# Output's first tile and first weight block prepared during attention's last steps, and one meeting of engines per stage change

## The reference, cut to what matters

```
h = concat(meta, x)                                  # 2064 x 1024
u = rms_norm(h) * norm_w
q, k, v, sb_gate, z, xbc, dt = split(u @ w_in)
o_sb  = stick_breaking_attention(q, k, v) * silu(sb_gate)
o_ssd = ssd_chunked(silu(conv(xbc)), dt, ...) * silu(z)
y = concat(rms_norm(o_sb) * sb_w, rms_norm(o_ssd) * ssd_w)   # 2048 wide
h = h + y @ w_out
out = rms_norm(h) * final_w                          # without the meta rows
```

## Time and profile before

| | us |
|---|---|
| median of 3 runs (2681.78 to 2683.33) | 2683.29 |
| the profiled execution, its own time | 2685.85 |
| its span, first to last instruction | 2683.9 |
| mean granted TensorE clock | 0.974 of full |
| PE busy | 2548.6 (95%) |
| DVE, ACT, POOL busy | 1688.8, 1347.1, 1552.1 |

### The profile page before, as it was taken

One profiled execution on the slowest core, in us unless ns is written; L12 is line 12 of the kernel. 1 busy time (PEld: TensorE's weight loads), 2 busy tenths in 40 slices (PEclk: granted clock), 3 DMA queues, 4 the chain that ended last, 5 costly groups with the idle time before them and its releaser, 6 DMA issues. The chain is left out here.

```text
span 2683.9 us, 41154 instructions
## 1 busy us (share of the span) xinstructions
PE 2548.6 (95%) x14100; PEld 1797.4 (67%) x14100; DVE 1688.8 (63%) x2064; ACT 1347.1 (50%) x2096; POOL 1552.1 (58%) x1253
## 2 busy tenths in 40 slices
PE   4999999998999999899899999999999999599998
PEld 3788777776888888766555555555555555488887
DVE  5522556635213455177688889888888987655554
ACT  4433333344333333344378778777877876322221
POOL 5876666688777777578666666565666655000000
PEclk7999999998999999999899999999999999799999
DMA  2443323333333333266712121212212111523230
GB/s 106 157 139 123 126 97 119 108 103 120 133 125 112 128 122 130 75 158 183 230 40 80 40 88 36 84 56 64 80 40 88 32 40 52 168 88 111 79 111 35
DMA packets 204101, 268.74 MB, mean 100 GB/s; under 512 B 13441, under 2 KB 137665, under 8 KB 197265
## 3 DMA queue, kind: packets, MB, share of 16 engines
q1 hardware_dynamic: 203920, 266.43, 31.0%
HBM read 169.36 MB, written 97.03 MB: 99 GB/s over the span
## 5 line engine op out<-in xcount | busy, mean ns | idle before, releaser
L2012 POOL TENSOR_TENSOR a_w<-a_beta,a_rest 128x1024 f32<-128x1024 f32 (+2 forms) x320 | 560.4, 1751 | 355.5 <-DVE a_rest L1969 209.3
L764 POOL TENSOR_TENSOR f_l_lo<-f_wst,f_l_hi 128x512 fp32r<-128x512 f32 x312 | 405.3, 1302 | 269.1 <-ACT f_l_hi L632 268.8
L1969 DVE TENSOR_TENSOR_SCAN a_rest<-a_keep,a_rest,a_ones 128x513 f32<-128x513 f32 x384 | 469.7, 1260 | 10.8 <-ACT a_keep L1939 10.8
L1889 PE MATMUL a_turn<-a_ident,a_w 128*128 128x128 f32 (+1 forms) x2432 | 343.6, 279 | 7.3 <-DVE a_wt L1923 6.1
L1904 PE MATMUL a_o<-a_wt,a_v 128*64 128x512 f32 (+3 forms) x1408 | 340.3, 562 | 8.9 <-DVE a_out L1979 8.9
L500 PE MATMUL f_xz<-f_t_hi,f_l_hi 128*128 128x512 f32 x832 | 330.2, 397 | 7.0 <-issue 4.4
L1923 ACT COPY a_wt<-a_turn 128x512 f32<-128x512 f32 (+3 forms) x440 | 225.1, 528 | 209.2 <-PE a_turn L1889 207.6
L500 PE MATMUL f_xz<-f_t_hi,f_l_lo 128*128 128x512 f32 x832 | 326.4, 392 | 0.0
L500 PE MATMUL f_xz<-f_t_lo,f_l_hi 128*128 128x512 f32 x832 | 326.0, 392 | 0.0
L1889 PEld LDWEIGHTS a_turn<-a_ident,a_w 128*128 128x128 f32 (+1 forms) x2432 | 257.6, 140 | 91.5 <-issue 65.4
L1939 ACT ACTIVATE a_keep<-a_z 128x1024 f32<-128x1024 f32 (+4 forms) x352 | 300.0, 852 | 4.5 <-PE a_z L1872 4.5
(11 more groups left out here) (256 smaller groups left out, 4272.5 us busy)
## 6 DMA issues: line engine op xcount, KB each, us to landing
f_wst<-in_w_pairs SPq DMA_DIRECT2D x52, 1024.0 KB, 5.8
scratch_gate<-f_out SPq DMA_DIRECT2D x64, 256.0 KB, 2.4
o_g<-scratch_mixed SPq DMA_DIRECT2D x32, 512.0 KB, 5.5
scratch_xbc<-f_out SPq DMA_DIRECT2D x36, 256.0 KB, 2.1
scratch_q_hi<-f_out SPq DMA_DIRECT2D x32, 256.0 KB, 3.3
scratch_q_lo<-f_out SPq DMA_DIRECT2D x32, 256.0 KB, 3.7
scratch_v<-f_out SPq DMA_DIRECT2D x32, 256.0 KB, 2.3
s_xc<-scratch_xbc SPq DMA_DIRECT2D x16, 512.0 KB, 5.8
```

Source lines behind the costliest of these rows:

```text
L764: return nc.gpsimd.tensor_tensor(out, a, b, op).then_inc(done, 1)
L1889: mm = nc.tensor.transpose(turn[h][0:rows, qi * P:(qi + 1) * P], tile[:, h, x:x + rows], ident[:, :])
L1969: mm = nc.vector.tensor_tensor_scan(rest[r % RS][:, h, tn - 1::-1], top, ones[:, 0:1].to_broadcast([P, tn]), start, ALU.mult, ALU.min)
L2012: nc.gpsimd.tensor_tensor(w[r % AS][:, :, 0:tn], beta[r % KEEPS][:, :, 0:tn], rest[r % RS][:, :, 1:tn + 1], ALU.mult).then_inc(w_ready, 1)
```

## The change

- **Meetings.** `start` no longer ends in a barrier: each engine raises its share and goes on; POOL then clears the semaphores that former stages left behind (`Memory.past`). At a stage's end they are only put on that list; the front stage alone (`at_once`) still clears and meets at its end. After output a clear and a meeting stand once.
- **Tile 0 of output in attention.** `OutputEarly` gets the tiles for it: high and low parts of g, a sum tile, the norm weights, high and low parts of one weight block. In the steps after the last score ACT squares the two halves (into the fourth staging tile) and takes a weight block's high part and both halves' high parts; DVE sums the two halves and takes the weight block's low part; POOL, after its last weights, multiplies both halves by the norm weights and takes their low parts. SP loads three weight blocks early instead of four, the norm weights with them, and two more blocks after the last chunk's store.
- **Order of weights.** Blocks come in the order 8 to 15, 0 to 7 (`place`), g's halves in the order 1, 0, and the first tile's products likewise. Block 8 is the one prepared early.
- **Output's opening.** Blocks 1 to 15 in that order; ACT squares tile 1 after the ninth, all else of tile 1's front comes after the last block, and its sums over blocks after `back(0, 0)`. Each half has its own `squares` tile.
- **Sums of squares** on PE stand between the first and second 48 matmuls of a tile, but for tile 0.

```
+    past = []
+
+    def __init__(self, nc, ctx, at_once=False):
+        self.nc, self.ctx, self.semaphores, self.at_once = nc, ctx, [], at_once
+        ctx.callback(self.leave)
 
     def start(self):
 
@@ -62,11 +64,21 @@
         engines = (nc.sync, nc.gpsimd, nc.scalar, nc.vector, nc.tensor)
         for n, sem in enumerate(self.semaphores):
             engines[n % len(engines)].sem_inc(sem, START)
-        nc.all_engine_barrier()
-
-    def clear(self):
-        self.nc.clear_and_free_semaphores(self.semaphores)
-        self.nc.all_engine_barrier()
+        Memory.clear(nc)
+
+    def leave(self):
+
+        Memory.past.extend(self.semaphores)
+        if self.at_once:
+            Memory.clear(self.nc)
+            self.nc.all_engine_barrier()
+
+    @staticmethod
+    def clear(nc):
+
+        if Memory.past:
+            nc.clear_and_free_semaphores(Memory.past)
+        Memory.past = []
...
-        m_ = Memory(nc, ctx)
+        m_ = Memory(nc, ctx, at_once=True)
...
                     late.load_first(sp)
+            sp.wait_ge(late.reduced[0][0], 1)
+            late.load_weight(sp, len(late.staging) - 1)
+            sp.wait_ge(late.w_high, 1)
+            sp.wait_ge(late.w_low, 1)
+            late.load_weight(sp, len(late.staging))
             for r in range(2):
                 sp.wait_ge(stored[r], START + 16 * CH // 2)
...
                 if n < N:
                     sigmoids(n)
+                if n == N:
+                    late.square(act, 1)
+                if n == N + 1:
+                    late.weight_high(act)
+                if n == N + 2:
+                    late.square(act, 0)
+                if n == N + 3:
+                    late.high(act, 1)
+                if n == N + 5:
+                    late.high(act, 0)
...
+                if n == N:
+                    late.reduce(dve, 1)
+                if n == N + 2:
+                    late.weight_low(dve)
+                if n == N + 3:
+                    late.reduce(dve, 0)
...
+            late.weigh(pool, 1)
+            late.weigh(pool, 0)
+            late.low(pool, 1)
+            late.low(pool, 0)
...
+        self.staging = self.h + self.y
+        self.squares = self.staging[-1]
         self.w_loaded = self.sems("o_w_loaded", len(self.staging))
...
+    def load_weight(self, sp, j):
+        r = j % len(self.staging)
+        sp.dma_start(self.staging[r][:, :], self.w_out[:, (j + KB) % MB, :]).then_inc(self.w_loaded[r], 16)
 
     def load_weights(self, sp):
-        for k in range(len(self.staging)):
-            self.load_weight(sp, k)
+        sp.dma_start(self.gw[:, :], self.group_w).then_inc(self.gw_loaded, 16)
+        for j in range(len(self.staging) - 1):
+            self.load_weight(sp, j)
 
     def load_g(self, sp, s, i):
-        for q in range(2):
+        for q in (1, 0):
...
+    def square(self, act, q):
+        act.wait_ge(self.g_loaded[0][q], 16)
+        if q == 0:
+            act.wait_ge(self.reduced[0][1], 1)
+        self.nc.scalar.activation(self.squares[:, :], self.half_of(self.g[0], q).rearrange("p b t -> p (b t)"), ACT.Square).then_inc(self.squared[0][q], 1)
+
+    def weight_high(self, act):
+        act.wait_ge(self.w_loaded[0], 16)
+        self.nc.scalar.activation(self.first_hi[:, :], self.staging[0][:, :], ACT.Copy).then_inc(self.w_high, 1)
+
+    def weight_low(self, dve):
+        dve.wait_ge(self.w_high, 1)
+        self.nc.vector.tensor_tensor(self.first_lo[:, :], self.staging[0][:, :], self.first_hi[:, :].bitcast(F32),
+                                     ALU.subtract).then_inc(self.w_low, 1)
+
+    def reduce(self, dve, q):
+        dve.wait_ge(self.squared[0][q], 1)
+        self.nc.vector.tensor_reduce(self.sq_sum[0][:, q, :],
+                                     self.squares[:, :].rearrange("p (b t) -> p t b", b=KB),
+                                     mybir.AxisListType.X, ALU.add).then_inc(self.reduced[0][q], 1)
+
+    def weigh(self, pool, q):
+        pool.wait_ge(self.gw_loaded, 16)
+        pool.wait_ge(self.squared[0][q], 1)
+        self.nc.gpsimd.tensor_tensor(self.half_of(self.g[0], q), self.half_of(self.g[0], q),
+                                     spread(self.gw[:, q * KB:(q + 1) * KB], P),
+                                     ALU.mult).then_inc(self.ssd_weighed if q else self.weighed[0], 1)
+
+    def high(self, act, q):
+        act.wait_ge(self.ssd_weighed if q else self.weighed[0], 1)
+        self.nc.scalar.activation(self.half_of(self.g_hi[0], q), self.half_of(self.g[0], q),
+                                  ACT.Copy).then_inc(self.ssd_high if q else self.g_high[0], 1)
+
+    def low(self, pool, q):
+        pool.wait_ge(self.ssd_weighed if q else self.weighed[0], 1)
+        pool.wait_ge(self.ssd_high if q else self.g_high[0], 1)
+        self.nc.gpsimd.tensor_tensor(self.half_of(self.g_lo[0], q), self.half_of(self.g[0], q),
+                                     self.half_of(self.g_hi[0], q).bitcast(F32), ALU.subtract).then_inc(self.ssd_low if q else self.g_low[0], 1)
...
+        squares = [m.sbuf(f"o_squares{q}", [P, D]) for q in range(2)]
...
+        def place(k):
+
+            return (k - KB) % MB
+
+        def weight(first, later, k):
+
+            return later[:, place(k) - 1, :] if place(k) else first[:, :]
+
+        def pipeline(eng, front, back, opening):
+
+            opening()
 
             def body(i, more):
                 if not (isinstance(i, int) and i == 0):
                     front(1, i)
-                back(0, i)
+                    back(0, i)
...
-            sp.dma_start(gw[:, :], group_w).then_inc(gw_loaded, 16)
             early.load_g(sp, 1, 0)
-            for k in range(STAGES, MB):
-                sp.wait_ge(w_high, k - STAGES + 1 + START)
-                sp.wait_ge(w_low, k - STAGES + 1 + START)
-                early.load_weight(sp, k)
-            sp.wait_ge(w_high, MB + START)
-            sp.wait_ge(w_low, MB + START)
-            for s in range(2):
-                load_h(s, 0)
+            for j in range(STAGES + 1, MB + 2):
+                sp.wait_ge(w_high, j - STAGES + 1 + START)
+                sp.wait_ge(w_low, j - STAGES + 1 + START)
+                if j < MB:
+                    early.load_weight(sp, j)
+                else:
+                    load_h(j - MB, 0)
...
+            def sums_of_squares(s, i):
                 pe.wait_ge(var_ready[1 - s], i + s + START)
                 for q in range(2):
                     pe.wait_ge(reduced[s][q], i + 1 + START)
                     last = nc.tensor.matmul(pss[:, q:q + 1], sq_sum[s][:, q, :], ones[:, :], start=True, stop=True)
                 last.then_inc(ssq_ready[s], 1)
+
+            def product(s, n, q, k):
+                cols = slice(n * W, (n + 1) * W)
+                hi, lo = weight(early.first_hi, later_hi, k), weight(early.first_lo, later_lo, k)
+                for lhs, rhs in ((g_hi, hi), (g_hi, lo), (g_lo, hi)):
+                    mm = nc.tensor.matmul(acc[n][q][:, :], lhs[s][:, k, :], rhs[:, cols],
+                                          start=(k == q * KB and lhs is g_hi and rhs is hi),
+                                          stop=(k == (q + 1) * KB - 1 and lhs is g_lo))
+                if k == (q + 1) * KB - 1:
+                    mm.then_inc(acc_ready[s][n][q], 1)
+
+            def opening():
+                pe.wait_ge(g_high[0], START + 1)
+                pe.wait_ge(early.ssd_low, START + 1)
+                pe.wait_ge(g_low[0], START + 1)
+                sums_of_squares(0, 0)
+                for q in (1, 0):
+                    for k in range(q * KB, (q + 1) * KB):
+                        pe.wait_ge(w_high, place(k) + 1 + START)
+                        pe.wait_ge(w_low, place(k) + 1 + START)
+                        for n in range(NH):
+                            product(0, n, q, k)
+
+            def back(s, i):
                 pe.wait_ge(g_high[s], i + 1 + START)
                 pe.wait_ge(g_low[s], i + 1 + START)
-
-                def product(n, q, k):
-                    for lhs, rhs in ((g_hi, w_hi), (g_hi, w_lo), (g_lo, w_hi)):
-                        mm = nc.tensor.matmul(acc[n][q][:, :], lhs[s][:, k, :], rhs[:, k, n * W:(n + 1) * W],
-                                              start=(k == q * KB and lhs is g_hi and rhs is w_hi),
-                                              stop=(k == (q + 1) * KB - 1 and lhs is g_lo))
-                    if k == (q + 1) * KB - 1:
-                        mm.then_inc(acc_ready[s][n][q], 1)
-
-                if isinstance(i, int) and i == 0 and s == 0:
-
+                for n in range(NH):
+                    pe.wait_ge(added[1 - s][n], i + s + START)
                     for q in range(2):
                         for k in range(q * KB, (q + 1) * KB):
-                            pe.wait_ge(w_high, k + 1 + START)
-                            pe.wait_ge(w_low, k + 1 + START)
-                            for n in range(NH):
```

(50 more changed lines are left out.)

86 lines of the change are left out of this document (42 added, 44 removed).

## The result

| | before | after |
|---|---|---|
| median of 6 runs each | 2683.31 | 2664.43 |
| ratio, 95% interval | | 0.9933 (0.992 to 0.9945) |
| span of the profiled execution | 2683.9 | 2663.2 |
| granted clock | 0.974 | 0.98 |

The change saves 18.9 us by the medians and 20.7 by the two traces. I had forecast 25.7 saved. The direction holds, and so does the mechanism of the opening; the size does not, and one loss, in the pace of the later tiles, was at nothing in my sum. By the ratio the kernel stands at 2665.3, just above my range of 2651 to 2665; its median, 2664.4, stands just inside. The page's second part answers to the earlier trace rows: the slice of the late change is 7 now, where it was 5.

The account below looks back on a forecast made before the run. PE was taken as busy except in the opening, stage changes and a late slice, where DVE, ACT and weight loads set the chain. −4.7 + 1.5 − 22.5 = −25.7 from a median of 2683.29 gave 2657.6, range 2651 to 2665.

Parts of the forecast that it names:

- Stage changes: Kernel start, front to scan, scan to attention: engines no longer wait for PE's semaphore raising; −1.4, −1.9, −1.4, together −4.7 us.
- T0: Clock origin of the sum: the moment attention's closing meeting lets the engines go, 2282.9 in the kernel before.
- Attention's last steps: End of attention: added work on DVE makes two evacuations late and PE loses 0.5 and 0.9 us; +1.5 in all.
- The opening: Output, from attention's closing meeting to tile 1: tile 0 prepared early, weight blocks uninterrupted; 35.0 us instead of 57.5, −22.5.
- From tile 1 on: Output's later tiles: same matmuls and sums, DVE has room, so a tile stays at 22.27 us; change nothing.
- a tile of over 22.3 us: Sign named beforehand, in output's later tiles: a tile longer than this would prove the prediction wrong.
- the moved sums: Rival, output's tiles: sums halfway make PE wait for DVE; 2 us a tile would give 2687.6; slower than before, chance 0.04.
- Slow loads or tail: Rival, output's opening: 6 us a landing, 4 us in attention's tail; 2660 to 2665; chance 0.14.
- the meetings give nothing: Rival, stage changes: each stage's first instructions still wait for a semaphore that PE raises last; 2662.3; chance 0.08.
- the idle time only moves: Rival, output's opening: tile 1's front still stops the weights and reduces stay on the path; 2672.5; chance 0.04.
- My estimate from the Trainium skill: Output's opening: 3.2 us for a block's load, rounds of 5.7, total 2.5 to 3 us lower than the forecast.

Follow-up runs that it names:

- seven_aligned: Changed kernel with seven staging tiles, tile 1's parts prepared amid the weight blocks, and the norm weights' tile widened from 64 to 512 bytes: 2652.04, ratio 0.9881.
- low_parts_shifted: Kernel before with the s = 0 tiles' g parts placed ahead of the weight tiles and an unused 64-byte tile between them: 2682.68 (one run).
- sums_first: Changed kernel with the sums of squares back ahead of a tile's 96 matmuls, for all tiles but the first two: 2664.85, ratio 0.9926.
- the padded kernel: Changed kernel with the norm weights' tile widened from 64 to 128 bytes a partition: 2664.42, ratio 0.9922.
- before_mid: Kernel before with the sums of squares between a tile's first and second 48 matmuls, for all tiles but the first: 2684.04 (one run).

## Why the prediction was right or wrong

- **Stage changes, −4.7.** Right in its parts: start about −1.5 for −1.4, scan −1.9 for −1.9, attention −1.6 for −1.4. With the meeting that opens output (in my opening's term) the run with them alone gave −4.8 by its ratio, −8.8 by its trace. With the tail's +1.5 my T0 was to come 3.2 us sooner; it came 4.5 sooner in the pair of traces, and 4.7 in the mean of the twelve traces of the changed kernel and its variants against seven of the kernel before and its own (2277.3 against 2282.0). Of the 1.3 to 1.5 us above my sum the three parts hold 0.3; the rest lies in the stages' own lengths, and no run explains it.
- **Attention's last steps, +1.5.** The places were right, the size 0.8, since DVE caught up in a step each time. By luck it is made good by the step that I costed at nothing: the two weight loads in flight with the last store, +0.8. I had weighed their issues, not their bytes.
- **The opening, −22.5.** The mechanism was right (slots, not DVE, set the pace, and PE never does), the size was −19.7. The blocks' end came at T0+28.8 instead of 26.9, mainly the landing taken at 4.5 us: the first, with tile 1's two loads of g beside it, took 5.72, the next 5.24 and 4.96. And 1.05 us of variance and power were left out. They stood before DVE's first addition already, but hidden: in the kernel before they ran right behind the last block, from 2334.34 to 2335.35, while the load of h for tile 0, issued at 2334.50, landed only at 2338.72, and the first addition followed that landing.

```profile
2334.34 0.15 DVE L2259 TENSOR_SCALAR o_var<-o_pss 128x2 f32<-128x2 f32 x1
2338.80 0.75 DVE L2266 SCALAR_TENSOR_TENSOR o_y<-o_acc,o_rstd,o_h 128x512 f32<-128x512 f32 x1 [4.31 <-issue]
```

  The change puts tile 1's parts, some 6.5 us, between the last block and this addition. It also issues that load sooner, at 2303.37, so nothing is left for the variance and the power, in order behind the parts, to hide under.
- **From tile 1 on, "Nothing".** This is the step that failed outright, and the largest miss, +3.3 us, of which 2.9 are the pace: with the operands aligned again, seven_aligned gave 2.85 back. The step counted the same instructions at the same duration and looked for waits alone. The duration itself changed through where a 64-byte tile was put, and 96 matmuls took 22.10 and 22.15 us instead of 21.93. I named "a tile of over 22.3 us" as what would prove me wrong; it did, though not by the rival that I had for it (the moved sums, 22.27 when tried alone).
- **The rivals.** "Slow loads or tail" has the right size, 2660 to 2665, but only half the reason. That the meetings give nothing, and that the idle time only moves, both fell. My estimate from the Trainium skill, "DMA: Bandwidth & Descriptors", would have had tile 1 at T0+32 to T0+32.5; the landings of 4.96 to 5.72 in the chain stand against its 3.2 for a block, a figure that the page fits to single transfers issued by GpSimd ("Anatomy of one DMA — SWDGE (gpsimd) path").
- **The sum against the medians.** The profiled execution before stood 2.5 above its median, that after 0.5 above: 20.7 saved between the traces are 18.9 between the medians. Executions of one kernel differ by a few us through front and attention, which a sum from one trace inherits.

## What to carry to other kernels

When work is taken off a chain, list everything between the last surviving producer and the first consumer again, the smallest instructions too: what was hidden behind a wait that the change removes comes out. Small tiles allocated between large matmul operands shift one against the other; round them up to 256 bytes a partition, and watch the time of a fixed number of matmuls from build to build. A stretch in which loads and one engine alternate has holes: put the next tile's preparation into them, and give the loads more slots before you call the transfer rate a limit.

## What the runs showed of the hardware

- The pace of full-clock 512-column matmuls depends on the two operands' relative place within a partition: apart by a multiple of 512 bytes, or by 256 more than one, 96 in 21.93 us; 64 bytes apart, 22.09 in low_parts_shifted and 22.34 in sums_first; the padded kernel, 128 apart for half of them, 22.17 to 22.24. Why is open, and so is why the same 64 bytes cost more than twice as much in sums_first; no run looked below 64 bytes or between 128 and 256.
- In tiles that run at 0.227 us a matmul, some ten behind the sums of squares are up to 9 ns slower, except in the s = 1 tiles of low_parts_shifted, where 96 took 21.88. These follow a slow tile; that the pace settles from where it was is my reading, and no run tests it.
- A DMA busy share of 0.97 was no full queue: 352 GB/s at 0.97, 420 at 1.03 with more transfers in flight.
- With 7.7 us between the starts of two neighbouring matmuls PE's next 48 took 12.80, with the granted clock at 0.50 in their first 2.7 us; with 1.5 us between them, 11.20 at 1.00. In before_mid 3.6 us were enough for the slow start: 12.62.
